# A two-layer hybrid decoder trunk on one core: input loads, the last gate sum, token turns and the gather's operands rearranged

## The reference

```
proj = h @ w_in                      # 1024 -> 6688 columns
y_a  = gated short convolution, y_b = latent attention with 8 heads and rotary key,
y_c  = convolution of 31 taps, LayerNorm, swish
x += (sigmoid(ga)*y_a + sigmoid(gb)*y_b + sigmoid(gc)*y_c) @ w_o
x += HierMoE(RMSNorm(x))             # best of 4 groups, 2 of its 8 experts, 32 experts in all
x += sigmoid(RMSNorm(x) @ w_ple_gate) * (p[i] @ w_ple)
```

## Time and profile before

| what | value |
|---|---|
| runs | 1144.97, 1145.93, 1146.28 us, median 1145.93 |
| the profiled execution, its own time | 1145.49 us |
| its span | 1143.7 us |
| mean clock granted to TensorE | 0.994 |
| busy: PE, PEld, DVE, ACT, POOL | 95%, 75%, 57%, 31%, 12% |
| moved by DMA | 300.39 MB, mean 263 GB/s, 411 to 420 in the expert stages |

### The profile page before, as it was taken

One profiled execution on the slowest core, in us unless ns is written; L12 is line 12 of the kernel. 1 busy time (PEld: TensorE's weight loads), 2 busy tenths in 40 slices (PEclk: granted clock), 3 DMA queues, 4 the chain that ended last, 5 costly groups with the idle time before them and its releaser, 6 DMA issues. The chain is left out here.

```text
span 1143.7 us, 21367 instructions
## 1 busy us (share of the span) xinstructions
PE 1088.4 (95%) x8168; PEld 857.6 (75%) x8168; DVE 649.0 (57%) x1353; ACT 356.1 (31%) x600; POOL 134.8 (12%) x163
## 2 busy tenths in 40 slices
PE   5999999999999999998989999999999999999986
PEld 5988998998765555554889799999887555555556
DVE  6687997455543333333777789965436333333356
ACT  4345442333421111111553454422334111111143
POOL 0121320011000100010002032101101001000000
PEclk9999999999999999999999999999999999999998
DMA  7558974546289999999454777654644999999952
GB/s 207 132 158 252 310 236 133 164 144 189 111 318 413 416 419 417 417 418 340 132 149 129 242 244 232 206 169 127 182 143 168 399 417 418 417 417 418 418 190 95
DMA packets 202981, 300.39 MB, mean 263 GB/s; under 512 B 14000, under 2 KB 166544, under 8 KB 186512
## 3 DMA queue, kind: packets, MB, share of 16 engines
q1 hardware_dynamic: 202896, 299.28, 73.8%
HBM read 298.21 MB, written 1.05 MB: 262 GB/s over the span
## 5 line engine op out<-in xcount | busy, mean ns | idle before, releaser
L732 PE MATMUL ps<-h_pair,wsplit 128*128 128x256 f32 x2880 | 368.4, 287 | 15.2 <-DVE h_pair L1834 7.4
L732 PEld LDWEIGHTS ps<-h_pair,wsplit 128*128 128x128 f32 x2880 | 354.6, 193 | 23.3 <-issue 14.0
L1825 DVE TENSOR_TENSOR wsplit<-ring,wsplit 128x1024 fp32r<-128x1024 f32 x136 | 167.4, 1235 | 64.4 <-ACT wsplit L1284 61.5
L1284 ACT ACTIVATE wsplit<-ring 128x1024 fp32r<-128x1024 f32 x136 | 141.5, 1055 | 197.6 <-PE ps L732 113.9
L732 PE MATMUL ps<-gu_ring,hT 128*64 128x256 f32 x896 | 107.6, 383 | 2.8 <-DMA gu_ring<-in_w_exp_up_dram 2.8
L1947 DVE SCALAR_TENSOR_TENSOR work<-work,convT 128x256 f32<-128x256 f32 x240 | 104.6, 507 | 0.0
L1511 ACT ACTIVATE prow<-ps 128x128 f32<-128x128 f32 x64 | 17.8, 278 | 278.7 <-PE ps L732 278.7
L2237 DVE TENSOR_TENSOR hT_r<-ps,hT_r 128x512 fp32r<-128x512 f32 x64 | 44.3, 692 | 93.6 <-ACT hT_r L1284 93.6
L732 PEld LDWEIGHTS ps<-gu_ring,hT 128*64 128x64 f32 x896 | 61.7, 137 | 47.4 <-issue 13.7
L2223 DVE TENSOR_TENSOR prow<-prow,ps 128x128 f32<-128x128 f32 x64 | 18.5, 288 | 131.6 <-ACT prow L1511 131.6
L1708 POOL COPY hT<-work 128x512 f32 x62 | 38.1, 615 | 403.6 <-PE ps L732 365.5
(11 more groups left out here) (213 smaller groups left out, 1149.9 us busy)
## 6 DMA issues: line engine op xcount, KB each, us to landing
ring<-in_w_in_dram SPq DMA_DIRECT2D x104, 512.0 KB, 4.6
down_ring<-in_w_exp_down_dram SPq DMA_DIRECT2D x40, 1024.0 KB, 19.7
gu_ring<-in_w_exp_gate_dram SPq DMA_DIRECT2D x28, 1024.0 KB, 15.1
gu_ring<-in_w_exp_up_dram SPq DMA_DIRECT2D x28, 1024.0 KB, 17.6
lent_down<-in_w_exp_down_dram SPq DMA_DIRECT2D x24, 1024.0 KB, 20.2
gu_last<-in_w_exp_gate_dram SPq DMA_DIRECT2D x12, 1024.0 KB, 14.4
gu_last<-in_w_exp_up_dram SPq DMA_DIRECT2D x12, 1024.0 KB, 16.8
ring<-in_w_exp_gate_dram SPq DMA_DIRECT2D x12, 1024.0 KB, 15.1
```

The lines of the kernel that those rows point to most:

```text
L732: return nc.tensor.matmul(o, lhsT, rhs, start=first, stop=last)
L1284: return nc.scalar.activation(o, i, ACT.Copy)
L1825: TT(tile_split[:, m, 1, :, :], tile_of(name, m), tile_split[:, m, 0, :, :].bitcast(F32), ALU.subtract).then_inc(tile_low, 1)
```

## The change

- SyncE issues x ahead of the vectors. TensorE turns the vectors in the middle of x's transposes. ScalarE takes all four pairs of x. VectorE does the last six rope steps behind unit q0, ScalarE sine and cosine behind the tiles of q2. Row and weight splits of the first unit are interleaved.
- VectorE adds the third branch for the last pair of chunks of `merged`.
- `tokens_of(m-1)` runs between the halves of unit wo`m`, not behind it.
- ScalarE writes the scaled tokens twice, rounded to `h_high` and plain to `hT`; GpSimd subtracts the two, in place, into `hT_r`, which shares `hT`'s memory. The selection gets tiles of its own, `choice`, over `prow` and `pT`, and its scratch lies over `bc` and `bcs`.
- The down part and the up part of expert 4 are loaded ahead of the gather, the gate part behind it.
- The list of window ends is spread behind the first half of expert 0's gate and up. The first window's first copy waits for the whole gather.

```diff
+            choice = [rounded_p.enter_context(nc.sbuf_tensor(f"choice{t}", [P, PAIRS], F32R)) for t in range(TC)]
...
-        h_tok = [... for h in (h_high, h_low)]
-        sel = wsplit[:, 1, 0, :, :]
+        h_tok = [... for h in (h_high, hT_r)]
+        sel_t = rows_bc[:, :, :].rearrange("p a n -> p (a n)")
...
+            sp.dma_start(xin, x[0].rearrange("(t q) d -> q t d", q=P)).then_inc(x_loaded, 16)
             load_vectors(0)
-            sp.dma_start(xin, x[0].rearrange("(t q) d -> q t d", q=P)).then_inc(x_loaded, 16)
...
                 load_down(l, OWN, OWN)
+                load_down(l, OWN + 1, OWN + 1)
+                load_gate_up(l, OWN + 1, OWN + 1, (1,))
                 sp.wait_ge(gather_psum, DC)
                 sp.sem_inc(wait_carried, 1)
-                load_gate_up(l, OWN + 1, OWN + 1)
-                load_down(l, OWN + 1, OWN + 1)
+                load_gate_up(l, OWN + 1, OWN + 1, (0,))
...
             for c in range(DC):
+                if c == DC // 2:
+                    turn_vectors(0)
...
-                for m in range(4):
-                    project_split(f"wo{m}", "wo" if m == 0 else None, late=2 if m == 0 else 0)
+                def between_halves(m):
...
-                    if m >= 1:
-                        tokens_of(m - 1)
+                    tokens_of(m - 1)
+
+                project_split("wo0", "wo", late=2)
+                for m in range(1, 4):
+                    project_split(f"wo{m}", between=lambda: between_halves(m))
                 tokens_of(3)
...
+                        if not ending:
+                            gate_up(it, k, 0)
                         if k == 0:
                             spread_ends()
-                        if not ending:
-                            gate_up(it, k, 0)
...
+                    take_x(0)
+                    take_x(1)
                     copy_vectors(0)
-                    high_tiles(l, "kv")
-                    high_rows(hT, [(h_ready[l], 2 * i + 2) for i in range(4)])
+                    take_x(2)
+                    take_x(3)
+                    rows_of = [(h_ready[l], 2 * i + 2) for i in range(4)]
+                    high_rows(hT, rows_of, range(2))
+                    high_tile(l, "kv", 0)
+                    high_rows(hT, rows_of, range(2, 4))
+                    high_tile(l, "kv", 1)
...
                 for i in range(4):
-                    nc.scalar.activation(two(h_tok[0][:, i // 2, (i % 2) * 512:(i % 2 + 1) * 512]), tokens(i), ACT.Copy,
-                                         scale=rms[:, 1, i // 2:i // 2 + 1]).then_inc(tok_high, 1)
+                    scaled_tokens(h_tok[0], i, tok_high)
+                    scaled_tokens(hT[:, :, :].rearrange("p c n -> p (c n)").rearrange("p (t d) -> p t d", t=TC), i, tok_high)
...
-                for m in range(4):
+                for m in range(3):
                     g = gate_t[m % 2]
                     pool.wait_ge(merge_step[l], m + 1)
...
                 power("ffn")
+                for i in range(4):
+                    pool.wait_ge(tok_high, 2 * i + 2)
+                    at = slice(i * 512, (i + 1) * 512)
+                    nc.gpsimd.tensor_tensor(hT_r[:, :, :].rearrange("p c n -> p (c n)")[:, at], hflat[:, at],
+                                            h_high[:, :, :].rearrange("p c n -> p (c n)")[:, at].bitcast(F32), ALU.subtract).then_inc(tok_low, 1)
...
                 take("q0", qn[:, 0:2, :])
+                if l == 0:
+                    rope_angles()
                 low_tile(l, "q1", 1)
...
-                low_tiles(l, "wo0")
+                dve.wait_ge(merge_step[l], 4)
+                wait_evacuated(dve, l, "yc3")
+                TT(merged[:, 6:8, :], merged[:, 6:8, :], two(gate_t[1][:, 2, :]), ALU.add).then_inc(merge_step[l], 1)
+                low_tile(l, "wo0", 0)
                 low_rows(merged, "wo", [3])
+                low_tile(l, "wo0", 1)
...
-                for i in range(4):
-                    dve.wait_ge(tok_high, i + 1)
-                    at = slice((i % 2) * 512, (i % 2 + 1) * 512)
-                    STT(two(h_tok[1][:, i // 2, at]), tokens(i), rms[:, 1, i // 2:i // 2 + 1], two(h_tok[0][:, i // 2, at].bitcast(F32)),
-                        ALU.mult, ALU.subtract).then_inc(tok_low, 1)
-
...
+                dve.wait_ge(p_ready, 1)
+                wait_unit(dve, l, "pp3")
                 for t in range(TC):
-                    step(TS(sel_t[:, t, :], iota, pos[0][:, t, :], None, ALU.is_equal))
-                    STT(sel[:, t, :], iota, pos[1][:, t, :], sel_t[:, t, :], ALU.is_equal, ALU.add).then_inc(sel_ready, 1)
+                    if t > 0:
+                        dve.wait_ge(sel_ready, t)
+                    step(TS(sel_t, iota, pos[0][:, t, :], None, ALU.is_equal))
+                    STT(choice[t][:, :], iota, pos[1][:, t, :], sel_t, ALU.is_equal, ALU.add).then_inc(sel_ready, 1)
...
                     for half in range(2):
+                        if half == 0:
+                            dve.wait_ge(gather_psum, DC)
                         dve.wait_ge(xs_read, 4 * half + 4)
```

More of the change, by code:

```diff
@@ L201, in program @@
         w_kr = sb("w_kr", [P, DC, QK])
+        with ExitStack() as rounded_p:
+            choice = [rounded_p.enter_context(nc.sbuf_tensor(f"choice{t}", [P, PAIRS], F32R)) for t in range(TC)]
         prow = sb("prow", [P, TC, S])
@@ L1291, in squares @@
                     nc.scalar.activation(dst[:, 2 * i:2 * i + 2, :], src[:, 2 * i:2 * i + 2, :], ACT.Square).then_inc(sq_ready[l], 1)
[L1293 to L1300, removed]
             def high_tile(l, name, m):
@@ L1471, in _ @@
                 wait_unit(act, l, "gc3")
-                high_rows(merged, [(merged_ready, i + 1) for i in range(4)], range(3))
+                high_rows(merged, [(merged_ready, i + 1) for i in range(3)], range(3))
                 high_tiles(l, "wo0")
-                high_rows(merged, [(merged_ready, i + 1) for i in range(4)], [3])
+                high_rows(merged, {3: (merge_step[l], 5)}, [3])
                 for m in range(1, 4):
@@ L1489, in _, with scaled_tokens @@
                 act.wait_ge(pow_ready[l], after(POWS, "ffn"))
+                def scaled_tokens(dst, i, done):
+                    nc.scalar.activation(two(dst[:, i // 2, (i % 2) * 512:(i % 2 + 1) * 512]), tokens(i), ACT.Copy,
+                                         scale=rms[:, 1, i // 2:i // 2 + 1]).then_inc(done, 1)
                 for i in range(4):
-                    nc.scalar.activation(two(h_tok[0][:, i // 2, (i % 2) * 512:(i % 2 + 1) * 512]), tokens(i), ACT.Copy,
-                                         scale=rms[:, 1, i // 2:i // 2 + 1]).then_inc(tok_high, 1)
+                    scaled_tokens(h_tok[0], i, tok_high)
+                    scaled_tokens(hT[:, :, :].rearrange("p c n -> p (c n)").rearrange("p (t d) -> p t d", t=TC), i, tok_high)
                 def take_embedded(m):
@@ L1755, in _, with rope_angles @@
             rstep(TS(a1, a1, ROUND, None, ALU.subtract))
-            rstep(STT(a0, a1, -TWO_PI[0], a0, ALU.mult, ALU.add))
-            rstep(STT(a0, a1, -TWO_PI[1], a0, ALU.mult, ALU.add))
-            rstep(STT(a0, a1, -TWO_PI[2], a0, ALU.mult, ALU.add))
-            rstep(TS(A, a0, PI_IN, -PI_IN, ALU.min, ALU.max))
-            rstep(STT(a2, A, -1.0, A, ALU.mult, ALU.min))
-            rstep(TS(a2, a2, HALF_PI, None, ALU.add))
-            for i in range(2):
-                dve.wait_ge(x_tr, 2 * i + 2)
-                nc.vector.tensor_copy(xT[:, 4 * i + 2:4 * i + 4, :], ps[:, 2 * i + 1, :]).then_inc(x_in, 1)
+            def rope_angles():
+                rstep(STT(a0, a1, -TWO_PI[0], a0, ALU.mult, ALU.add))
+                rstep(STT(a0, a1, -TWO_PI[1], a0, ALU.mult, ALU.add))
+                rstep(STT(a0, a1, -TWO_PI[2], a0, ALU.mult, ALU.add))
+                rstep(TS(A, a0, PI_IN, -PI_IN, ALU.min, ALU.max))
+                rstep(STT(a2, A, -1.0, A, ALU.mult, ALU.min))
+                rstep(TS(a2, a2, HALF_PI, None, ALU.add))
             def add_square_pair(l, name, sq, i):
@@ L1861, in _ @@
                 if l == 0:
-                    low_rows(hT, "mix")
-                    low_tiles(l, "kv")
+                    low_rows(hT, "mix", range(2))
+                    low_tile(l, "kv", 0)
+                    low_rows(hT, "mix", range(2, 4))
+                    low_tile(l, "kv", 1)
                     add_square_pair(l, "mix", sq_x, 1)
@@ L2189, in weigh_slots @@
                         TS(gw[:, t, :], iota, pos[0][:, t, :], weight[0][:, t, :], ALU.is_equal, ALU.mult)
-                        step(TS(sel_t[:, t, :], iota, pos[1][:, t, :], weight[1][:, t, :], ALU.is_equal, ALU.mult))
-                        TT(gw[:, t, :], gw[:, t, :], sel_t[:, t, :], ALU.add).then_inc(gw_ready, 1)
+                        if t > 0:
+                            dve.wait_ge(gw_ready, t)
+                        step(TS(sel_t, iota, pos[1][:, t, :], weight[1][:, t, :], ALU.is_equal, ALU.mult))
```

(3 more changed lines are left out.)

30 lines of the change are left out of this document (17 added, 13 removed).

## The result

| kernel | median (lowest to highest), us | ratio to before, 95% interval |
|---|---|---|
| before | 1146.11 (1144.97 to 1146.58) | |
| changed | 1156.99 (1156.19 to 1158.60) | 1.0096 [1.0084, 1.0108] |

The change costs 10.9 us. Slower was forecast; the size was not, and the result lies above the range. The profiled execution of the changed kernel took 1158.6 us (span 1156.5, mean clock 0.986). That is 13.1 above the profiled execution of before, 2.2 more than the medians differ by.

The account below looks back on a forecast made before the run. TensorE, busy for 95% of the span, was taken as the bound. Per layer +2.45, twice +4.9, start -2.45 and clock +2.0 gave +4.45 on 1145.49: 1149.9 us, range 1141.0 to 1153.5.

Parts of the forecast that it names:

- the start: Start of the kernel: x sooner -2.4, interleaved splits -0.8, later rope steps +0.75, in sum -2.45 us, once.
- the clock: Routing: more TensorE idle time brings low clock, slowing embedding 3 and matmuls next to it, +2.0 us in one layer.
- the low part on GpSimd: Routing: GpSimd's four subtractions each hold up VectorE's chain by 0.87 us, +3.5 us a layer.
- The upper bound 3.0, the lower 1.8: Start: bounds in us on the gain from issuing x ahead of the vector loads; 2.4 was taken.
- a stall of 1.7 is there to win: First projection: 72 matmuls took 10.59 us instead of 8.9; interleaving the splits was to win 0.8 of it.
- the rope term: Start: six rope steps moved behind the first q unit delay a weight split on VectorE, costing 0.75 us.
- The last rival: Routing: stalls of 4.8 us a layer and low clock in both layers, 1154.5 us in all; chance 0.1.
- The rival in which the small operations slip between: Routing: GpSimd's adds cost VectorE's chain little, 1140.9 us in all, faster; chance 0.2.
- Choosing: Last count to released gather: VectorE's removed work mostly replaced by a wait for embedding 3, -0.65 us a layer.
- Gate sum: Last gate sum on VectorE instead of GpSimd: TensorE goes on sooner, -1.3 us a layer.
- tokens: Output projection's end: token turns between halves no longer cover the last addition to x, +0.9 us a layer.
- early loads and list ends: Around the gather: expert 4's loads sent sooner and the list-ends matmul moved, each worth 0.

Follow-up runs that it names:

- low_on_vector: The changed kernel with the low part of the tokens made by VectorE again, new memory places kept: 1144.57 us, ratio 0.9990.
- gpsimd_later: The changed kernel with GpSimd's four subtractions waiting until VectorE's routing chain is over: 1150.83 us, ratio 1.0042.
- warm_routing: The changed kernel with five dummy matmuls on TensorE ahead of its wait for the first count: 1150.83 us, ratio 1.0046.
- x_first_alone: The kernel before with only the x load issued ahead of the nine vector loads: 1146.49 us, ratio 0.9998.
- sum_alone: The kernel before with only the last gate sum moved to VectorE: 1141.25 us, ratio 0.9966.
- sum_x_first: The kernel before with the last gate sum on VectorE and x loaded ahead of the vectors: 1142.36 us, ratio 0.9967.
- sum_loads_late: The kernel before with the last gate sum on VectorE and the later list ends, expert 4 loaded wholly behind the gather: 1142.98 us, ratio 0.9978.

## Why the prediction was wrong

The direction and most of the steps stood. Three terms were mis-sized, all to the same side: the start, the clock and, by less, the low part on GpSimd.

**Start, forecast -2.45, profile +1.63, over the profiles about 0: the step that failed most.** It had two mistakes. The first is x: "The upper bound 3.0, the lower 1.8" took the time at which a load is issued for the time at which it lands, less 1.2 for the constants. x's transposes were to begin at 7.7 and began at 9.74; the runs showed 0.4 sooner on average and 0.8 at best. I had counted what lies ahead of x, and left out that x now shares full queues with it and with the vectors. The windows show the full queues; no run takes the constants or the vectors away, so how the lost 2.6 divides between them stays open. The second is "a stall of 1.7 is there to win", from 72 matmuls in 10.59 us instead of 8.9. There was no stall. TensorE waited for nothing among those matmuls and ran the first 3.9 us of them at half pace, which interleaving the splits cannot change, and which the start's sum has no term for.

The +1.63 of the profile is: x used 0.41 sooner, the way from there to the first projection 0.67 shorter, a new wait of 0.50 for the second pair of rows, a wait of 0.68 for the late weight split (the rope term, forecast 0.75, which was right), and 1.5 for half pace until 24.5 instead of 21.7; together +1.6. The two waits of 2.67 and 0.50 that took the place of one of 3.53 gained 0.36 of the 0.8 that I had put on interleaving.

**Clock, forecast +2.0 once, measured +2.2 in each layer.** The mechanism and its size for one layer were right: the idle time grew from 0.9 to 4.79, embedding 3 was slow, and it was on the path. "In one layer of the two" was wrong: I took the frequency from before, where layer 1 had it and layer 0 not, though the wait that I forecast stands in both. Of eight stretches behind such a wait, in four profiles, all eight were low. This step is +2.4 of the error. The last rival, stalls and clock in full, had low clock in both layers; at 1154.5 it came nearest and was given 0.1. Its 4.8 of stalls a layer did not come.

**Low part on GpSimd, forecast +3.5 a layer, measured +3.88.** The price of one hold was too low, 0.96 to 1.12 instead of 0.87 for three of the four. The steps of the chain add up: 1.13 - 0.17, 2.44 - 0.29, 0.97 - 0.22 and 0.58 - 0.22 are 4.22. Before, the chain already lost some to GpSimd's 1.49 operation, which ran earlier; low_on_vector shows it:

```profile
299.20 1.50 POOL L1708 TENSOR_SCALAR work_r<-cst 128x512 fp32r<-128x512 f32 x1
...
299.42 0.41 DVE L2139 TENSOR_TENSOR work<-work 128x8 f32<-128x8 f32 x1
...
300.46 0.26 DVE L2151 TENSOR_SCALAR work<-work 128x8 f32<-128x8 f32 x1
```

Those are 0.24 and 0.09, and 4.22 - 0.33 = 3.89. The rival in which the small operations slip between fell.

The reading of "one small operation, or two" after each release was right: it was the held one, and once a reduction with it. The Trainium skill ("SBUF — State Buffer", section "Who interferes with whom") says which ones are held: VectorE instructions with two inputs in SBUF, and copies, casts and tensor_scalar in a two-port mode, but no reductions and none with at most one input there outside those modes. The held operation of the earlier trace rows, which the prediction set beside the rule for two inputs, is a tensor_scalar and falls under the second half. The trace agrees with the page: the reduction at 304.82 took its 0.22 inside GpSimd's block, and with an input in PSUM the one at 305.46 in gpsimd_later took 0.23.

**Choosing, forecast -0.65, measured +1.5 with the clock's cost in it, and -0.7 without.** Before, 13.51 and 13.49; in warm_routing, at full clock, 12.82 and 12.80. The changed kernel's count to released gather is 317.44 - 310.03 = 7.41; warm_routing's is 5.22, against 5.27 forecast.

**Gate sum, -1.3 against -1.39; tokens, +0.9 against +1.06; early loads and list ends, 0 against 0.** These were right, and so were the first two reasons: the second split is late next, and unit 3's add lost its cover. That the expert stage takes its pace from TensorE's progress fits, but was not tested by itself. The -0.86 of the table is no gain of the loads: x_first_alone and sum_alone, whose experts run as before, take 0.5 to 1.3 less a layer as well.

**The sum against the profiles.** The one profile of the changed kernel has the late end of the slow pace in full. Start +4.1 over the forecast; the clock +2.4; contention 2 x 0.38 = +0.8; gate sum and tokens +0.1; choosing -0.1; experts -0.9. That is +6.4 on 4.45, 10.8. The remaining 2.1 of the 13.0 lie behind the experts, in stretches that the diff does not touch. In layer 0, 1.29 of it is a stretch at half clock from 557 to 560 us. Six of the fourteen profiles have it, three of them with the old chain (x_first_alone, sum_x_first, sum_loads_late), and they take 53.75 to 54.19 from the experts to the next key matmul; the eight without take 51.09 to 52.50. So it comes and goes whatever the kernel.

**The sum against the medians.** With the start at about 0 instead of -2.45, the clock at +4.4 and contention at +7.8, the forecast's sum becomes +10.1, against 10.9 measured. The last 0.8 is within what the intervals leave open.

## What to carry to other kernels

Work moved from VectorE to GpSimd was paid by VectorE here, once for each large operation that met its dependent chain: count the operations that run beside the chain, not those removed from VectorE. The wait of 4.8 us ahead of matmuls on the path had two prices, its length and the slow matmuls behind it, in every layer that had it; a few dummy matmuls in the hole told the two apart. An earlier issue is worth the earlier landing only, here 0.4 of 3.0. Matmuls that take longer than they should are not always waiting: count them in windows before calling the difference a stall, and do not trust a clock of 1.00 ahead of the trace's first record of it.

## What the runs showed of the hardware

- Beside a GpSimd operation of 128x512 with two inputs, a VectorE operation on 8 columns took 1.13 us instead of 0.17, and a run of four such GpSimd operations held four VectorE operations, one each, to its own end. GpSimd's four took 4.95 to 5.12. Beside GpSimd's tensor_scalar of 128x512 (1.49 us) the loss was less, 0.09 to 0.36.
- A hole of 4.79 us in TensorE's work was followed by 6.8 us at the 1.2 GHz level, some of it still in the hole, which cost 1.6 to 2.2 us; with dummies in the hole there was none.
- x, issued 3.0 us sooner behind the same constants, took 7.4 to 8.2 us to be of use instead of 5.1 to 5.2.
- The first projection ran at half pace for 3 to 7 us in thirteen of fourteen profiles, also where the trace has no record of the clock, and at full pace with dummies ahead of it.
- Behind the experts the clock fell for 3.4 us in some profiles and not in others of like kernels. One profile is then 1 to 3 us off its kernel's median, as large as most of the terms here.
